# Transposes of two tiles moved from ScalarE copies and VectorE blocks to TensorE, in a one-core Mamba, gMLP and MoE layer

## The reference, cut to what matters

```python
h = rms_norm(x, norm1_g)
z, xbc, dt_raw, gu, gv = split(h @ w_in)
xbc_act = silu(causal_conv(xbc))            # 1024 channels, width 4
xs, bm, cm = split(xbc_act)                 # 512 of x, 256 of B, 256 of C
y = ssd_scan(xs, dt, a, bm, cm) + xs * d_skip
ssd_out = group_rms_norm(y * silu(z))       # 512 columns
gmlp_out = gelu(gu) * (tril(w_s) @ layer_norm(gelu(gv)) + b)   # 512 columns
x = x + concat(ssd_out, gmlp_out) @ w_out
x = x + hier_moe(rms_norm(x, norm2_g))      # top-1 of 4 groups, top-2 of 8 experts
```

## Time and profile before

| | |
|---|---|
| median of three runs | 2790.24 us (2789.75 to 2790.36) |
| profiled execution | 2790.36 us, of which the span from the first to the last instruction is 2788.5 us |
| phase 1 up to the end of turn 0 | until 139.5 us (up to turn 1's `ydiag` and states) |
| turns 1 to 31, up to the first product of turn 31's output projection | 139.5 to 1858.7 us |
| phase 2, from its first expert product | 1923.1 us to the end |
| mean granted clock of TensorE | 0.991 of 2.4 GHz |

### The profile page before, as it was taken

How to read it: one execution, slowest core, us unless ns; L and a number is a source line. 1 busy time by engine, 2 the same in 40 slices (tenths; PEclk the granted TensorE clock), 3 DMA queues, 4 the chain that set the end, 5 groups by cost and what they waited for, 6 DMA issues and landing times.

```text
span 2788.5 us, 38529 instructions
## 1 busy us (share of the span) xinstructions
PE 2737.2 (98%) x11715; PEld 1768.6 (63%) x11715; DVE 1883.0 (68%) x5154; ACT 1454.7 (52%) x3396; POOL 818.0 (29%) x1368
## 2 busy tenths in 40 slices
PE   8999999999999999999999999997999999999997
PEld 6777677767776777677767776763444444444443
DVE  5776767676767676767676767665666666666665
ACT  2445544454455444544454445434666666666665
POOL 1121112111211121112111111112556555556555
PEclk9999999999999999999999999998999999999999
DMA  7311111111111111111111111156888677778864
GB/s 305 136 64 46 69 67 48 46 69 61 54 46 69 64 51 46 69 59 56 46 69 61 54 46 61 42 199 252 307 291 294 236 274 255 280 258 293 317 215 146
DMA packets 104914, 377.91 MB, mean 136 GB/s; under 512 B 32713, under 2 KB 34642, under 8 KB 94706
## 3 DMA queue, kind: packets, MB, share of 16 engines
q1 hardware_dynamic: 44226, 236.13, 23.1%
q0 software_dynamic: 60480, 139.24, 14.8%
HBM read 326.14 MB, written 123.03 MB: 161 GB/s over the span
## 4 chain that ended last, share of the span: by engine, by line
PE 95%; DMA 2%; DVE 1%; ACT 1%; issue 1%; SPq 0%; POOL 0%; POOLq 0%; DVEq 0%; ACTq 0%
PE PB L367 24%; PE PB L1659 20%; PE PB L378 16%; PE PB L457 12%; PE SS L1678 5%; PE TB L1678 5%; PE YB L457 4%; PE YB L411 2%; DMA arena<-in_w_in 1%; PE SS L420 1%; PE SS L424 1%; PE TB L433 1%; PE YB L1669 1%; PE MB L402 1%; PE YB L515 0%
## 5 line engine op out<-in xcount | busy, mean ns | idle before, releaser
L367 PE MATMUL PB<-arena,hT 128*128 128x512 f32 (+2 forms) x2112 | 728.3, 498 | 1.8 <-ACT xT L590 1.1
L1659 PE MATMUL PB<-arena,hT 128*128 x1296 | 582.5, 592 | 0.0
L367 PEld LDWEIGHTS PB<-arena,hT 128*128 128x128 f32 x2112 | 396.7, 190 | 276.9 <-issue 229.7
L378 PE MATMUL PB<-hT,arena 128*128 128x128 f32 x4224 | 487.5, 276 | 4.7 <-DVE arena L1148 4.6
L378 PEld LDWEIGHTS PB<-hT,arena 128*128 128x128 f32 x4224 | 481.8, 193 | 8.9 <-issue 4.9
L1659 PEld LDWEIGHTS PB<-arena,hT 128*128 128x128 f32 x1296 | 239.9, 190 | 271.2 <-issue 271.2
L1185 POOL TENSOR_SCALAR rs<-sq 128x2 f32<-128x2 f32 (+1 forms) x66 | 14.2, 216 | 1254.7 <-ACT h L750 910.3
L457 PE MATMUL PB<-arena,tT 128*128 128x274 f32 (+1 forms) x1056 | 361.6, 497 | 0.3 <-ACT tT L644 0.3
L457 PEld LDWEIGHTS PB<-arena,tT 128*128 128x128 f32 x1056 | 197.1, 192 | 142.7 <-issue 123.4
L636 ACT ACTIVATE yb<-ycat 32x128 f32<-32x128 f32 x768 | 235.9, 307 | 89.3 <-DVE ycat L933 48.7
L1789 DVE TENSOR_TENSOR gv<-ycat,PB 128x256 f32<-128x256 f32 x81 | 34.1, 421 | 290.1 <-ACT ycat L1741 280.8
(11 more groups left out here) (292 smaller groups left out, 4109.0 us busy)
## 6 DMA issues: line engine op xcount, KB each, us to landing
arena<-in_w_expert SPq DMA_DIRECT2D x32, 2048.0 KB
arena<-in_w_expert SPq DMA_DIRECT2D x32, 1024.0 KB
h_rows<-h SPq DMA_DIRECT2D x34, 512.0 KB, 2.8
x_in<-in_x_rows SPq DMA_DIRECT2D x33, 512.0 KB, 4.4
hT<-in_x_cols SPq DMA_DIRECT2D x33, 512.0 KB, 3.6
x_res<-in_x_rows SPq DMA_DIRECT2D x33, 512.0 KB, 4.2
dec<-running_sums SPq DMA_DIRECT2D x33, 512.0 KB, 3.6
x_rows<-x_res SPq DMA_DIRECT2D x33, 512.0 KB, 2.6
```

What stands on the lines that cost most here:

```text
L367: mm = nc.tensor.matmul(out, hT[u][:, k, :], w_group(name)[:, k, :], start=k == 0, stop=k == KD - 1)
L378: mm = nc.tensor.matmul(PB[b][:, c * P:(c + 1) * P], w_block(name, c)[:, k, :], hT[u][:, k, :], start=k == 0, stop=k == KD - 1)
L1659: mm = nc.tensor.matmul(PB[u][:, :], hT[u][:, k, :], arena[:, bass.ds(slot + k * 2 * DE, 2 * DE)], start=k == 0, stop=k == KD - 1)
```

## The change

Both transposes go to TensorE. In every turn `pe_turned(i)` stands between `pe_front_sums` and the projection `z`, and `act_turned(i)` behind ScalarE's copy of the running sums. `pe_front_channels` begins with six transposes of `xc` into `TB[0]` (four) and `TB[1]` (two), and `act_front` with two copies out of them into `xtok` and `btok`, which take the place of `xbtok`. `act_move_rows`, `act_move_channels`, `dve_turn_rows` and the transposes of `dve_front` are gone. `pe_out` waits for both halves of `tT` ahead of its first product, where it had waited for each half ahead of the four products that use it.

```diff
@@ pe_front_channels @@
             pe.wait_ge(s["xc_ready"], t + 1)
+            after(pe, s["ycT_out"], 2 * t)
+            for b in range(2):
+                for k in range(4 - 2 * b):
+                    mm = nc.tensor.transpose(TB[b][:, k, :], xc[:, 4 * b + k, :], ident)
+                mm.then_inc(s["xb_full"], 1)
             pe.wait_ge(s["acs_out"], t + 1)
@@ pe_mix_pair; pe_mix_sample waits for xb_out, 2 * NP + 1, where it waited for ycat_hi @@
             pe.wait_ge(s["v_ready"], i + 2)
+            pe.wait_ge(s["xb_out"], 2 * i + 2)
@@ pe_turned @@
-            transpose8(pe, block_of(ycat), lambda b: [("ycat_hi", i + 1)], "ycT_full")
+            transpose8(pe, block_of(ycat), lambda b: [("ycat_hi", i + 1)] if b == 0 else [("xb_out", 2 * i + 2)], "ycT_full")
@@ pe_out @@
+            pe.wait_ge(s["ycT_out"], 2 * (i + 1))
             pe.wait_ge(*free)
             for k in range(KD):
-                if k % 4 == 0:
-                    pe.wait_ge(s["ycT_out"], 2 * i + 1 + k // 4)
@@ pe_turn @@
             pe_front_sums(pe, i + 1)
+            pe_turned(pe, i)
             project(pe, v, PB[1][:, :], "z", "proj_z", [("xb_evicted", i + 2)])
...
-                pe_spread(pe, i + 2, TB[0], [("ycat_hi", i + 1)])
+                pe_spread(pe, i + 2, TB[0], [("xb_out", 2 * i + 3)])
@@ act_turned @@
-                act.wait_ge(s["ycT_full"], b + 1)
+                act.wait_ge(s["ycT_full"], 2 * i + 1 + b)
@@ act_silu @@
             nc.scalar.activation(xc[:, :, :], xc[:, :, :], ACT.Silu).then_inc(s["xc_ready"], 1)
-            act_move_channels(act, t)
@@ act_front @@
+            act.wait_ge(s["xb_full"], 2 * t + 1)
+            after(act, s["gated_ready"], t)
+            nc.scalar.activation(xtok[:, :], flat(TB[0][:, :, :]), ACT.Copy).then_inc(s["xb_out"], 1)
+            act.wait_ge(s["xb_full"], 2 * t + 2)
+            after(act, s["states_done"], t)
+            nc.scalar.activation(btok[:, :], flat(TB[1][:, 0:2, :]), ACT.Copy).then_inc(s["xb_out"], 1)
@@ act_turn @@
-                act_move_rows(act, i, 0)
...
-            act_move_rows(act, i, 1)
             act.wait_ge(s["proj_u"], i + 2)
+            act.wait_ge(s["ycat_hi"], i + 1)
             nc.scalar.activation(gu[:, :], PB[0][:, :], ACT.Gelu_apprx_tanh).then_inc(s["gu_out"], 1)
             act_sums(act, i + 1)
+            act_turned(act, i)
             act_silu(act, i + 1)
@@ dve_front @@
-            if t > 0:
-                dve.wait_ge(s["ycat_hi"], t)
-                dve_turn_rows(dve, t - 1, 1)
...
-            by_token = xbtok[:, :].rearrange("p (c g i) -> p g c i", g=4, i=32)
-            dve.wait_ge(s["xc_ready"], t + 1)
-            after(dve, s["states_done"], t)
-            for q in range(4):
-                V.transpose(by_token[32 * q:32 * (q + 1), 3, :, :], channels_quarter(3, q))
...
-            dve.wait_ge(s["xc_moved"], t + 1)
-            V.transpose(by_token[:, 0:2, :, :], tmp[:, 0:384].rearrange("p (g c t) -> p g c t", g=2, t=32))
-            V.transpose(by_token[:, 2, :, :], ycat[:, 0:192].rearrange("p (c t) -> p c t", t=32)).then_inc(s["xb_out"], 1)
-            dve.wait_ge(s["xb_out"], t + 1)
+            dve.wait_ge(s["xb_out"], 2 * (t + 1))
@@ dve_turn @@
-            dve_turn_rows(dve, i, 0)
             dve_mixed(dve, st, i)
             dve_conv(dve, st, i + 1)
```

More of the change, by code:

```diff
@@ L183, in build @@
         xc = sb("xc", [P, CB, P])
-        xbtok = sb("xbtok", [P, W + G * N])
-        xtok, btok = xbtok[:, 0:W], xbtok[:, W:]
+        xtok = sb("xtok", [P, W])
+        btok = sb("btok", [P, G * N])
         gu = sb("gu", [P, W])
@@ L260, in build @@
             proj_xa proj_xb proj_va proj_vb proj_u proj_z xa_out xb_evicted va_out gv_out gu_out z_out cache_set
-            halo_saved conv_done xc_ready cb_done xc_moved xb_out
+            halo_saved conv_done xc_ready cb_done xb_full xb_out
             dt_read lg_read cb_read rank_read dtneg_ready dtexp_ready dtrec_ready dt_ready acs_out sumT_done sumT_out
@@ L265, in build @@
             ydiag_done yoff_done states_done state_ready gated_ready ysq_ready yr_ready ycat_ready
-            ycT_full yc_moved ycT_out out0 out1 out2 x2_part x2sq_ready x2r_ready h2_ready
+            ycT_full ycT_out out0 out1 out2 x2_part x2sq_ready x2r_ready h2_ready
             gexin_ready gexout_ready pick_ready rank_done slots_ready
@@ L438, in pe_mix_sample @@
             pe.wait_ge(s["v_ready"], NT)
-            pe.wait_ge(s["ycat_hi"], NP)
+            pe.wait_ge(s["xb_out"], 2 * NP + 1)
             pe.wait_ge(s["ws_ready"], 2)
@@ L576, in pe_phase1 @@
             over_tiles(lambda tn: pe_turn(pe, tn))
-        channels_moved = [tmp[:, 0:192], tmp[:, 192:384], ycat[:, 0:192]]
         def act_channels(act, b, t, u, to_sample, done):
@@ L627, in act_sums @@
             nc.scalar.activation(sumT[:, :], sumT_p, ACT.Copy).then_inc(s["sumT_out"], 1)
[L629 to L634, removed]
-                for q in range(4):
-                    ins = nc.scalar.activation(yb[32 * q:32 * (q + 1), g * P:(g + 1) * P], rows_quarter(b, g, q), ACT.Copy)
-            ins.then_inc(s["yc_moved"], 1)
         def act_turned(act, i):
             for b in range(2):
-                act.wait_ge(s["ycT_full"], b + 1)
+                act.wait_ge(s["ycT_full"], 2 * i + 1 + b)
                 after(act, s["out2"], i)
                 nc.scalar.activation(tT[:, half(b), :], TB[b][:, :, :], ACT.Copy).then_inc(s["ycT_out"], 1)
[L646 to L651, removed]
-            if t > 0:
[L653 to L658, removed]
         def act_silu(act, t):
@@ L722, in act_turn @@
                 act_ysq(act, 0)
-                act_move_rows(act, 0, 0)
             else:
@@ L911, in dve_mixed @@
             V.tensor_tensor(ycat[:, W:], tmp[:, :], gu[:, :], ALU.mult).then_inc(s["ycat_hi"], 1)
[L913 to L926, removed]
         def dve_normed(dve, st, t):
```

## The result

The changed kernel took 2829.39 us, the median of four runs (2827.98 to 2830.60), against 2789.99 of the kernel before in its runs. The ratio is 1.0141, with a 95% interval of 1.0124 to 1.0158. It is slower by 39.4 us; 41.4 were forecast, and the forecast time was 2831.8. The profiled execution took 2827.62 us with a span of 2825.8, which is 37.3 over the span of before. A second profiled execution, taken later, took 2827.31 us with a span of 2825.5, so the two profiles agree with each other; the median of the timed runs lies 1.8 and 2.1 us above them.

What follows compares the result with a forecast made beforehand. TensorE was taken to bound the kernel, without a gap in turns 1 to 31. Terms 50.8 - 3.3 - 1.8 - 1.2 - 3.5 + 0.4 = +41.4 us on 2790.36 gave 2831.8 us, range 2828 to 2844.

Steps and rivals of the forecast that it cites:

- TensorE is the bound and has no room: Turns 1 to 31: TensorE busy 1708.96 of 1708.96 us; two waits touch the change, 3.3 and 1.2 us.
- The price of a transpose: TensorE's stream: 0.112 us for each of 454 transposes, 14 in a steady turn, 50.8 us in all.
- What ScalarE and VectorE lose: Copies and block transposes gone, 768 copies being 235.9 us; costed at nothing in turns 1 to 31.
- Turn 0: The 3.3 us wait for `xc_ready` goes, and 1.8 us of slow products behind it.
- Turn 31: The 1.2 us wait ahead of `ydiag` goes, and 3.5 us of slow clock behind it.
- The sample turn: `pe_out` waits for both halves of `tT`, costing 0.4 us more.
- The start: Ahead of turn 0's gating: six more transposes on TensorE make it 0.7 us later.
- Rival 1: Waits and slow clock in turns 0 and 31 not given back: +51.2 us, 2841.6; chance 0.25.
- rival 2: Clock falls in every turn, 3.5 us each, 112 us in all: 2944 us; chance 0.05.
- rival 3: A transpose costs a whole 32-bit product, two records, 0.223 us: +91.9, 2882.3 us; chance 0.05.
- rival 4: New TensorE wait each turn because ScalarE is late, 0.55 us, 17 in all: about 2849; chance 0.06.
- rival 5: Transposes cost next to nothing, hidden under 128 x 512 products; paybacks remain: 2781.0 us, faster; chance 0.04.

Runs made afterwards that it cites:

- e1_ycat: Kernel before, with only the transposes of `ycat` moved to TensorE, in every tile; those of `xc` stay on ScalarE and VectorE: 2807.60 us, ratio 1.0072.
- e2_xc: Kernel before, with the transposes of `xc` moved to TensorE in every tile, those of `ycat` only in tile 32: 2806.67 us, ratio 1.0068.
- e4_four: Changed kernel with every group of transposes issued four times over, writing the same values again: 2978.30 us, ratio 1.0682 to the kernel before.
- h1_edges: Kernel before, with TensorE transposing only `ycat` of tiles 0, 31 and 32 and `xc` of tile 32: 2782.66 us, ratio 0.9981.
- h2_edges: Kernel before, with TensorE transposing only `ycat` of tiles 0 and 32 and `xc` of tile 32: 2781.41 us, ratio 0.9976.
- e5_products: Changed kernel with each transpose issued as an ordinary 32-bit product against the identity: 2885.31 us, ratio 1.0348 to the kernel before.

## Why the prediction was right

**TensorE is the bound and has no room.** Right: no gap in turns 1 to 31 up to `z` of turn 31, before or after, and the two waits that were named have gone, with a third of 0.29 us.

**The price of a transpose.** Right: 14 in a turn were to take 1.57 us, and the two rows take 1.58. What the sum lacked is that `z` gets 0.10 us shorter when it no longer stands behind the sums, so the turn grew by 1.49, 0.106 for each transpose and 5% less than forecast. Over 30 turns that is 2.4 of the 4.1 us between forecast and profile. The duration of 0.27 to 0.28 us played no part: the trap was to multiply by it.

**What ScalarE and VectorE lose.** Right: worth nothing in a steady turn, and all that it pays back lies in turns 0 and 31. The spare time at `xc_ready` was 3.1 us against 3.2.

**Turn 0.** -3.8 against -3.5. The wait and the slowness behind it went. `e1_ycat` shows that the turning of `ycat` made the wait, `e2_xc` that the wait can come without the slowness. So of the 5.1 us counted back, 3.3 are shown to hang on the change; the other 1.8 are what this one profile of the kernel before happened to hold, and that they fitted is in part luck.

**Turn 31.** -3.6 against -3.1. It was the least sure term, and it came. 0.36 of it is the third wait (3.96 us from L537 to L542 before, 3.60 from L543 to L548 after), and 0.10 is `z`; neither was in the sum. The low clock went in `e1_ycat`, `e2_xc`, `e4_four`, `h1_edges` and `h2_edges` too. But that the pause brought it is not shown: `e1_ycat` has a pause of 0.46 us there and a clock of 1.00, and `e5_products` has no wait and takes 3.21 us for `ydiag` at a falling clock (0.79, then 0.50). So the clock can fall in this thin stretch without a pause, and the 3.5 us could have failed to come.

**The sample turn.** +0.4 as forecast.

**The start.** Forecast +0.7, measured -0.2. Neither the low clock at 64 us (some 1.6 us) nor a start-up that was 2.2 us shorter by the end of `u` was in the sum; that they partly cancel is luck. The largest part of what varies there is again the granted clock: the same projection `u`, begun between 41 and 42.1 us, took 7.13 us at 1.00 (`h2_edges`) and 10.15 us where the clock was 0.50 from 42 to 46 us (`h1_edges`), with the other profiles between them.

**The rivals.** Rival 1 (nothing given back) is refuted by turns 0 and 31; rival 2 (the clock falls in every turn) by the clock of 1.00 in the changed kernel and in the fourfold one; rival 3 (two records) by counts and prices; rival 4 (a new wait) did not come, beyond the 0.4 us; rival 5 (hidden) is refuted by 0.106 us a piece.

## What to carry to other kernels

Where one engine has no gap, ask of a change only what it puts on that engine, and price it by the distance between starts, not by an instruction's duration. Relief of the others pays only where the bound engine waits for them; find these places in its list of waits, and apply the change there and nowhere else. Here the whole change cost 39 us, and the two or three tiles of it that remove waits brought 6 to 7.

## What the runs showed of the hardware

- A 32-bit 128 x 128 transpose on TensorE is one record. Six in a row take 0.65 us up to the next start and 24 take 2.61, 0.108 to 0.109 each; eight ahead of `z` take 0.93 and 32 take 3.54, 0.116 and 0.111. As a product against the identity it is two records and costs 0.223. A single record of either lasts 0.27 to 0.28 us.
- The granted clock of TensorE held at 1.00 through 32 transposes in a row (3.5 us) between dense products. In tile 0's front it fell to 0.50 although TensorE had no gap there. Each time it fell at the end of a row of 32 records with 36 columns or just behind one, and was below 1.00 in three neighbouring windows of 2 us: in the changed kernel (from 64 us, twice), `e1_ycat` (72), `e2_xc` (72), `h2_edges` (62) and `e5_products` (72), with transposes near and without. It did not in the kernel before, in `h1_edges` or in `e4_four`, whose 24 transposes stand at that place. Every profile but that of `h2_edges` has one more such fall, between 38 and 48 us, at the end of the same kind of row or behind it, where a wait of 0.65 to 0.95 us lies too. What picks the place stays open.
- A 128 x 512 projection directly behind the two small sums took 0.10 us longer to the next start than behind transposes (6.97 and 6.87 us). The cause was not looked for.
